# The MLP's up projection in seven block products for eight, with its low parts made by VectorE and its relu and square by ScalarE

## What is computed

```
h2 = rms_norm(x, norm_mlp) * (1.0 + sc_m) + sh_m
x = x + g_m * (jnp.square(jax.nn.relu(h2 @ w_up)) @ w_down)
```

## Time and profile before

| | us |
|---|---|
| median of 3 runs | 1150.59 (1147.83 to 1153.65) |
| the profiled execution | 1152.23 |
| its span in the trace | 1150.4 |
| TensorE busy in the span | 1099.8 (96%) |
| VectorE busy | 682.5 (59%) |
| ScalarE busy | 487.3 (42%) |
| GpSimd busy | 88.1 (8%) |

### The profile page before, as it was taken

The page is one execution under the profiler, slowest core; times in us unless marked ns, Lnnn a source line. Parts: engine busy times, 40 slices in busy tenths (PEclk is TensorE's granted clock), DMA queues, the critical chain, the costliest instruction groups (busy, mean ns, idle before and its releaser), DMA issues.

```text
span 1150.4 us, 21500 instructions
## 1 busy us (share of the span) xinstructions
PE 1099.8 (96%) x8725; PEld 1041.6 (91%) x8725; DVE 682.5 (59%) x1512; ACT 487.3 (42%) x851; POOL 88.1 (8%) x65
## 2 busy tenths in 40 slices
PE   5899999998999999999999998899999999999997
PEld 4698889976999999999899998899999999999997
DVE  5736554444487877778875545637355563636465
ACT  3543556456544454643444224542323323242334
POOL 2400000000000000000000011420101001010101
PEclk9899999999999999999999999999999999999998
DMA  9884333212321313222222481222232223223202
GB/s 307 270 296 155 116 106 109 77 38 74 119 93 56 113 58 113 77 76 69 81 83 88 152 255 42 65 83 74 74 110 74 74 75 109 74 74 97 73 16 83
DMA packets 108775, 120.20 MB, mean 104 GB/s; under 512 B 2692, under 2 KB 98780, under 8 KB 108389
## 3 DMA queue, kind: packets, MB, share of 16 engines
q1 hardware_dynamic: 108677, 118.83, 32.2%
HBM read 108.99 MB, written 11.80 MB: 105 GB/s over the span
## 4 chain that ended last, share of the span: by engine, by line
PE 79%; DVE 11%; ACT 5%; issue 3%; DMA 1%; POOL 0%; SPq 0%; DVEq 0%; ACTq 0%; POOLq 0%
PE PS L847 59%; PE PS L802 4%; PE PS L956 2%; DVE wR L1403 2%; PE PS L820 2%; ACT wR L1086 1%; PE PS L793 1%; DVE xhat L1371 1%; PE PS L926 1%; PE PS L904 1%; PE PS L890 1%; ACT pr L1213 1%; DMA xn<-in_x_sample 1%; PE PS L769 1%; PE PS L996 1%
## 5 line engine op out<-in xcount | busy, mean ns | idle before, releaser
L847 PE MATMUL PS<-hR,wR 128*128 128x288 f32 x3744 | 523.5, 298 | 0.8 <-issue 0.8
L847 PEld LDWEIGHTS PS<-hR,wR 128*128 128x128 f32 x3744 | 502.7, 188 | 9.7 <-issue 8.8
L1403 DVE TENSOR_TENSOR wR<-raw,wR 128x512 fp32r<-128x512 f32 x260 | 203.1, 781 | 107.7 <-ACT wR L1086 100.2
L847 PE MATMUL PS<-actR,wR 128*128 128x288 f32 (+2 forms) x1920 | 260.9, 297 | 1.8 <-DVE actR L1545 1.8
L847 PEld LDWEIGHTS PS<-actR,wR 128*128 128x128 f32 x1920 | 257.0, 189 | 3.0 <-DVE actR L1545 2.0
L1086 ACT ACTIVATE wR<-raw 128x512 fp32r<-128x512 f32 x260 | 164.4, 632 | 140.6 <-PE PS L847 132.9
L1465 DVE CAST actR<-tmp 128x576 fp32r<-128x576 f32 x32 | 15.2, 476 | 125.8 <-ACT tmp L1197 125.8
L802 PE MATMUL PS<-wR,hR 128*128 128x256 f32 x600 | 77.5, 286 | 0.0
L802 PEld LDWEIGHTS PS<-wR,hR 128*128 128x128 f32 x600 | 73.4, 191 | 1.8 <-issue 1.7
L1420 DVE SCALAR_TENSOR_TENSOR xT<-PS,mods,xT 128x288 f32<-128x288 f32 x68 | 35.2, 518 | 62.8 <-PE PS L847 56.2
L1196 ACT ACTIVATE tmp<-PS 128x576 f32<-128x576 f32 x32 | 20.9, 652 | 120.0 <-PE PS L847 117.7
(11 more groups left out here) (219 smaller groups left out, 1066.1 us busy)
## 6 DMA issues: line engine op xcount, KB each, us to landing
raw<-in_w_in SPq DMA_DIRECT2D x30, 1024.0 KB, 5.2
raw<-in_w_up SPq DMA_DIRECT2D x16, 1024.0 KB, 5.4
raw<-in_w_down SPq DMA_DIRECT2D x16, 1024.0 KB, 5.1
mid<-in_w_ada SPq DMA_DIRECT2D x12, 1024.0 KB, 5.2
ada<-in_w_ada SPq DMA_DIRECT2D x8, 1024.0 KB, 12.0
S<-in_state_hgrn SPq DMA_DIRECT2D x8, 512.0 KB, 4.4
out_hgrn_sample<-S SPq DMA_DIRECT2D x8, 512.0 KB, 6.7
raw<-in_w_out SPq DMA_DIRECT2D x4, 1024.0 KB, 5.6
```

The costliest lines, as they stand in the source:

```text
L847: mm = pe.matmul(PS[:, 2 * x.pair + h, 0:size], weights(x, w, k, col), rhs[r], start=(k == 0 and n == 0), stop=(k == last and n == 2))
L1403: done(dve.tensor_tensor(w[:, 1, cols], raw[SLOT[SPLITS[n]]][:, cols], w[:, 0, cols].bitcast(F32), ALU.subtract), s_lo)
```

## The change

Up units 2 to 15 (the list SEVEN) are computed by a scheme of seven block products for eight. Such a unit is a product of 2 x 2 blocks of weights (W: two blocks of 128 outputs by two halves of the contraction) with 2 x 2 blocks of tokens (X: two halves of the contraction by two halves of the tokens). One block product is 12 matmuls of 288 columns, so a unit is 84 matmuls for 96. With S1 = W21+W22, S2 = S1-W11, S3 = W11-W21, S4 = W12-S2 and T1 = X12-X11, T2 = X22-T1, T3 = X22-X12, T4 = X21-T2, the products p0 to p6 are W11 X11, W12 X21, S2 T2, S1 T1, S3 T3, S4 X22 and W22 T4. p0, p2, p4 and p6 add up in one PSUM bank (A[0] for even units, A[3] for odd ones), p1 is in A[1], p3 and p5 are in A[2]. Between them the partial sums are copied out: TensorE starts p2 only when ScalarE has copied p0, p4 when it has copied p2, p5 when it has copied p3, and p6 when it has copied p4 (s_kept).

The T blocks are made once (combine, halve): four subtractions of 128 x 1152 on VectorE, four high parts on ScalarE and four low parts on VectorE. The weight sums are made per unit: four VectorE instructions of 128 x 512 (sums). A unit of this kind has seven high and seven low pieces for four. Taking it out is the work of seven(), squares_of() and low(): ScalarE makes four copies of 288 columns out of PSUM, relu, square and high part of the first half of the outputs (576 columns), two relus of 288, and a square and a high part for the second half; VectorE makes three additions of 288 columns and the two low parts in actR. GpSimd does nothing in these units. h2 is kept in float32 in xhat1.

The core of the diff (event loops, buffers and semaphores left out):

```diff
+SEVEN = [u for u, x in enumerate(UNITS) if x[0] == "up" and x[1] >= 2]
+PRODUCTS = [("11", "11", 0, True), ("12", "21", 1, True), ("S2", "T2", 0, False), ("S1", "T1", 2, True),
+            ("S3", "T3", 0, False), ("S4", "22", 2, False), ("22", "T4", 0, False)]
+PIECES = ["11", "12", "S1", "S3", "S2", "22", "S4"]
+WX = ["S3", "S2", "S4"]
+TX = ["T2", "T1", "T3", "T4"]
...
+            if squared is not None and c == 0:
+                yield ("low", squared, 0)
...
+            if x.kind == "up" and x.i == 0 and x.n == 0 and c == 3:
+                yield ("combine",)
+                yield ("halve", 0)
+                yield ("halve", 1)
+            if x.kind == "up" and x.i == 1 and x.n == 0 and c in (1, 3):
+                yield ("halve", 2 + c // 2)
+            if x.u in SEVEN:
+                yield ("seven", x, c)
+            if squared is not None and c == 0:
+                yield ("squared", squared)
+            elif squared is not None:
+                yield ("low", squared, 1)
+                squared = None
...
+            def product(x, c):
+                j = SEVEN.index(x.u)
+                wa, tb, i, start = PRODUCTS[c]
+                bank = bank_of(x, i)
+                pe.wait_ge(s_lo, cuts(x.split, PIECES.index(wa) + 1))
+                if j == 0 and c == 0:
+                    pe.wait_ge(s_dve_free, count_read(LAST[LATE[-1]], "dve"))
+                if j == 0 and tb in TX:
+                    pe.wait_ge(s_tlo, TX.index(tb) + 1)
+                if c == 0:
+                    if j >= 2:
+                        pe.wait_ge(s_kept, 5 * (j - 1))
+                elif c == 1:
+                    if j:
+                        pe.wait_ge(s_added, 3 * j - 2)
+                elif c == 3:
+                    if j:
+                        pe.wait_ge(s_added, 3 * j)
+                else:
+                    pe.wait_ge(s_kept, 5 * j + {2: 1, 4: 2, 5: 3, 6: 4}[c])
...
+                if u in SEVEN:
+                    b = PIECES[q]
+                    src, dst = piece(n, b)
+                    if b[0] == "S":
+                        act.wait_ge(s_sum, 4 * SEVEN.index(u) + ["S1", "S3", "S2", "S4"].index(b) + 1)
+                    if u == SEVEN[1] and b in WX or u == SEVEN[0] and b == "S4":
+                        act.wait_ge(s_tx, 4)
+                    done(act.activation(dst[0], src, ACT.Copy), s_hi)
+                    return
...
+            def halve(c):
+                act.wait_ge(s_tx, c + 1)
+                done(act.activation(tR[:, c, 0, :], tF[:, c, 1, :], ACT.Copy), s_thi)
+            def seven(x, c):
+                j = SEVEN.index(x.u)
+                if c == 1:
+                    return
+                if c == 5:
+                    act.wait_ge(s_added, 3 * j + 3)
+                    done(act.activation(tmp[0][:], tmp[0][:], ACT.Relu))
+                    squares_of(x, 0)
+                    return
+                bank = bank_of(x, PRODUCTS[c][2])
+                if c == 6:
+                    act.wait_ge(s_mm, x.t + 2)
+                    done(act.activation(halves_of(1)[0], bank[:, 0:HALF], ACT.Relu), s_kept)
+                    done(act.activation(halves_of(1)[1], halves_of(1)[1], ACT.Relu))
+                    return
+                act.wait_ge(s_prod, 6 * j + c + 1)
+                if j == 0:
+                    act.wait_ge(s_alo, 2 * x.i)
+                elif c == 0:
+                    act.wait_ge(s_rlo, 2 * j - 1)
+                elif c == 3:
+                    act.wait_ge(s_rlo, 2 * j)
+                dst = {0: (0, 0), 2: (0, 1), 3: (1, 0), 4: (1, 1)}[c]
+                done(act.activation(halves_of(dst[0])[dst[1]], bank[:, 0:HALF], ACT.Copy), s_kept)
+            def squares_of(x, n):
+                i = 2 * x.i + n
+                if i >= 8:
+                    act.wait_ge(s_mm, LAST[UNITS.index(("dn", 2 * (i // 4 - 2) + 1))] + 1)
+                done(act.activation(tmp[n][:], tmp[n][:], ACT.Square))
+                done(act.activation(actR[:, i // 4 % 2 * 4 + i % 4, 0, :], tmp[n][:], ACT.Copy), s_rhi)
...
+            def sums(n, q):
+                u = SPLITS[n]
+                w = raw[SLOT[u]][:]
+                one, three = columns(summed("S1")), columns(summed("S3"))
+                if q == 0:
+                    dve.wait_ge(s_raw[SLOT[u]], raw_loads(u))
+                    done(dve.tensor_tensor(one, cut(w, "21"), cut(w, "22"), ALU.add), s_sum)
+                    done(dve.tensor_tensor(three, cut(w, "11"), cut(w, "21"), ALU.subtract), s_sum)
+                elif q == 3:
+                    done(dve.tensor_tensor(one, one, cut(w, "11"), ALU.subtract), s_sum)
+                elif q == 5:
+                    done(dve.tensor_tensor(one, cut(w, "12"), one, ALU.subtract), s_sum)
+            def seven(x, c):
+                j = SEVEN.index(x.u)
+                if c == 1:
+                    to, add, kept = halves_of(0)[0], bank_of(x, 1)[:, 0:HALF], 1
+                elif c == 5:
+                    dve.wait_ge(s_kept, 5 * j + 4)
+                    done(dve.tensor_tensor(halves_of(1)[1], halves_of(1)[1], halves_of(1)[0], ALU.add), s_added)
+                    to, add, kept = halves_of(0)[1], bank_of(x, 2)[:, 0:HALF], 2
+                else:
+                    return
+                dve.wait_ge(s_prod, 6 * j + c + 1)
+                dve.wait_ge(s_kept, 5 * j + kept)
+                done(dve.tensor_tensor(to, to, add, ALU.add), s_added)
+            def low(x, n):
+                i = 2 * x.i + n
+                dve.wait_ge(s_rhi, 2 * SEVEN.index(x.u) + n + 1)
+                a_ = actR[:, i // 4 % 2 * 4 + i % 4]
+                done(dve.tensor_tensor(a_[:, 1, :], tmp[n][:], a_[:, 0, :].bitcast(F32), ALU.subtract), s_rlo)
```

131 lines of the change are left out of this document (112 added, 19 removed).

## The result

The changed kernel takes 1189.4 us (median; 1188.8 to 1190.6) against 1151.3: ratio 1.0335, 95% interval 1.0306 to 1.0363. It is slower. The forecast was 1186, range 1170 to 1201.

A forecast was written before the change was run, and what follows sets the result against it. TensorE alone was taken to bound the kernel. Group waits less saved matmuls (+13.8), clock falls (+11.9) and the entry (+9.35) gave +35 us on the profiled 1152.2: 1187, median 1186, range 1170 to 1201.

The forecast's parts named there:

- Bound and saving: In the MLP TensorE alone sets the pace; leaving out 168 matmuls of 0.133 us can gain 22.3 us at most.
- The seam: Between even and odd up unit, TensorE waits 3.3 us at p2 for ScalarE's copy of p0 into tmp0.
- The dn unit: In the first dn unit behind an odd up unit, the third tile waits 1.75 us for VectorE's residual.
- The clock: TensorE's clock falls after each odd unit's p2 wait, costing 1.7 us each time, seven times: +11.9 us.
- the rival with both waits falling: The dn unit's idle of 1.6 us brings the clock down too: another 11.9 us, 1197; chance 0.21.
- The entry: Once, at up 1 and up 2: +6.05 wait behind the T blocks, +2.3 clock, about +1 at up 2; sum +9.35.
- at up 2 the first copy waits for GpSimd's low part of up 1, about +1: At up 2, ScalarE's first copy is held up by GpSimd's low part of up 1: about 1 us.
- The sum: Whole kernel: 13.8 for waits less saved matmuls, 11.9 for clock, 9.35 for the entry: +35 us, median 1186.
- The rival "faster": The odd unit's p0 copy ends by 14.4 instead of 17.65: 1151, or 1138 without the dn wait; chance 0.08.
- the break-even of 1.85: Waiting and clock loss per group at which the kernel breaks even: (22.3 - 9.35) / 7 = 1.85 us.
- The rule cited for the low parts: In the new up units GpSimd is idle, so VectorE's low parts and weight sums take 0.69 us, not up to 1.96.
- The estimate for 1152 columns: At the entry, a T block's 128 x 1152 subtraction on VectorE takes 1.36 us, by a straight line between measured sizes.

The follow-up runs named there:

- e6: The kernel before the change with 12 of 96 matmuls skipped in each up unit from the third on, output lacking these products: 1126.8 us.
- e2: The changed kernel with the first half of even up units put into another SBUF buffer, rb, instead of tmp[0]: 1164.9 us.
- e5: The changed kernel with the activation's 28 low parts in the new up units made by GpSimd again instead of VectorE: 1166.4 us.
- e4: The changed kernel with the four weight pieces made during the first dn unit behind an odd up unit one tile later: 5.7 us less.
- e1: The changed kernel with the first two ScalarE high parts of the T blocks moved behind up 0's relus and squares: 1189.6 us.
- e3: e2 with ScalarE's copy of the odd unit's p0 moved directly behind relu, square and high part of the even unit's first half: 1166 us.
- e11: e8 plus three rotating buffers and a reordered entry, then four more order moves on ScalarE and VectorE; those four took 6.8 us off.
- e12: e11 with the odd unit's p3 copied earlier and the three buffers rotated in another order: 2.0 us less, 0.9927 of the kernel before the change.
- e7: e3 with ScalarE's copy of the odd unit's p2 also moved, ahead of two high parts of the dn unit's weight: gained nothing.
- e8: e7 with the four weight pieces in the first dn unit of groups 1 to 6 one tile later: 13 us less.

## Why the prediction was right

**Bound and saving.** Right: TensorE alone was the bound (rows 3), and 168 x 0.133 = 22.3 was the whole possible gain; e6 gave 23.

**The seam.** Right to 0.2 us in every link. Counted from p0 of the even unit at 978.36, ScalarE's relu began at 11.16 (11.2 forecast), the high part of S4 ended at 15.53 (15.6), the low part at 17.12 (17.1), the copy at 17.64 (17.65). The wait was 3.44 for 3.29. That the buffer was the last link is shown by e2. That its release was late since the low part stood behind VectorE's weight pieces is shown by e5.

**The dn unit.** The wait, 1.63 for 1.75, was right. The links were as forecast, in the order of the rows above: a weight's low part, the activation's, a weight's, the residual. That the weight pieces were among them is shown by e4. For the activation's low part there is the trace alone: e5 took it out, but put a stretch of 0.66 us in its place. 0.39 us behind the wait were not in the sum; the 0.12 ahead of it did not show.

**The clock.** Too high by 1.9. It did not fall each time: after the first seam's 3.29 us of idle it stayed at 1.00 (window at 778). The six others cost 1.2 to 2.7 us, on average the 1.7 taken, 10.0 together for 11.9. That an idle of 1.6 would not bring it down held in all seven groups; the rival with both waits falling is out. By the rule of the Trainium skill (Perfetto Trace Analysis, Matmul Optimizations) that matmuls should run back to back the change was at a disadvantage. The traces agree after six of the seven long idles.

**The entry.** The wait ahead of up 1 was 7.05 - 0.85 = 6.20 (6.05), its clock 2.03 (2.3). The step that was mis-sized is "at up 2 the first copy waits for GpSimd's low part of up 1, about +1": it was 2.8, and the idle then cost 1.5 of clock. The low part itself began late, since ScalarE's relu had stood behind a high part of up 2's weight for which VectorE was late, and GpSimd took 1.84 with VectorE working beside it. The forecast called VectorE's T work hidden. It was not: with up 1 started at once (e1), VectorE works without a gap from 735.4 and TensorE idles 10.01 us at up 2.

**The sum.** Forecast: 25.7 in the groups and 9.35 at the entry, +35. Measured: 25.9 (38.2 of waits, 10.0 of clock, less 22.3) and 12.5, +38.4 of the 38.8 found. The medians differ by 38.1, and the 3.4 us above the forecast are nearly all the entry's mis-sized step. That the groups' sum came out to 0.2 is luck in part: 1.9 too much for the clock stood against 2.1 too little for the waits, above all the 0.39 behind each dn wait.

**The rival "faster".** The forecast let it hang on one copy: in time, and the kernel takes 1151. In the changed kernel the copy was late, so the rival's condition was not met. But its price was wrong as well: in e3 the copy ends at 13.7, ahead of the 14.4 asked for, and the time is 1166, since the idle stands at p4 instead. With the copy early by 1.7 us (e2) a group keeps 51.73 - 47.88 = 3.85 us of waits, 1.8 at the seam and 2.0 at the dn unit, over the break-even of 1.85. Only e11 (1.1 left) and e12 (0.6) are past it.

**The rule cited for the low parts.** Weight pieces took 692 ns in the groups with GpSimd idle and 871 with it at work (e5), as the Trainium skill (SBUF — State Buffer, Who interferes with whom) has it for a VectorE instruction with two SBUF inputs beside a GpSimd instruction that reads SBUF. It spoke for the change, and taken alone it misled: the interference was real and even stood in the chain at the dn unit, but at the seam the parallel engine took a link out of the chain, and the kernel that kept it was 23 us faster.

**The estimate for 1152 columns.** 1.36 us, from rows 4. The formula of the Trainium skill (VectorE: DVE Perf Modes, The TRN2 errata) gave an estimate of 1.36 us too, and the T block's row above has 1.36.

## What to carry to other kernels

When work is taken off the bounding engine, write out the queue of each helper over one period and follow the chain of releases link by link; a busy share of 48 or 65% says nothing about it. Look first at which buffer a copy out of PSUM writes and who reads that last: one more buffer brought 24.6 us here. Moving a copy ahead in a queue that stayed as full (e3, e7) brought nothing, moving work to a place with room (e8) brought 13. An idle engine that takes one link in parallel can be worth more than it costs, 23 us here (e5); but look whether the instruction it slows stands in a chain itself, as at the dn unit.

## What the runs showed of the hardware

The price of an idle on TensorE does not follow from its length alone. Idles of 1.62 to 1.65 us between two products were followed by full clock in six groups of e2, six of e3 and all seven of e5, and those of 1.37 to 1.72 in the dn units in every kernel that had them; in the kernel before 1.76 was already enough for half clock (rows 8 and 9). Idles of 2.08 and 2.01 (first groups of e2 and e3) were followed by half clock, 1.2 GHz, and those of 3.3 in six of seven groups of the changed kernel and of e4. So halving the idle saved nearly as much again in clock: 1.5 of the 3.2 us a group in e2. But 2.39 us in e12 (770.32 above) was followed by full clock, and practically the same idle at up 2's p2, 2.94 and 2.95, kept the clock in e11 and lost it in e12. TensorE and a window of e11, then of e12:

```profile
753.64 1.87 PE L931 MATMUL PS<-tR,wx_S 128*128 128x288 f32 x12 [2.94 <-DVE wx_S L1634]
756.00:758.00 2.00, 2.00 (x17) 2.00 (x16) 0.83 (x2) 1.88 (x4) 0.00 (x0) 1.00 0.01 2
```
```profile
754.18 2.10 PE L935 MATMUL PS<-tR,wx_S 128*128 128x288 f32 x12 [2.95 <-DVE wx_S L1640]
756.00:758.00 2.00, 2.00 (x10) 2.00 (x9) 1.38 (x2) 1.86 (x4) 0.00 (x0) 0.50 0.00 0
```

After equal idles of 3.3 the loss ran from 0 to 2.7 us, and in the sixth group it was 1.5 in the changed kernel and 2.7 in e4, where only the dn wait was gone. What decides between these was not settled.

Two subtractions of 128x1152 on VectorE took 2.75 us with GpSimd idle (changed kernel) and 4.98 with GpSimd at work (e1). GpSimd's own 128x576 low part took 1.43 us on average in e5, and 1.84 beside VectorE at the entry of the changed kernel.
